# Eight PSUM banks of an attention stage dealt out anew: two for scores, three for maxima and transposed values

## The chip, the cores and the metric

The kernel runs on one core of one Trainium2 chip. The metric is the device time of the whole program in microseconds (us), the median of several runs.

## What is computed

One layer with two groups of heads over the same 2048 x 1024 input. Four heads are a gated DeltaNet (linear attention with a state that is carried from chunk to chunk); eight heads of 64 columns are forgetting attention. Both are gated, joined, projected out and normalised. The change concerns the attention alone:

```python
log_f = jax.nn.log_sigmoid(f_logit + f_bias)
cum = jnp.cumsum(jnp.moveaxis(log_f, 2, 1), axis=-1)
for i in range(s // Q_BLOCK):
    lo, hi = i * Q_BLOCK, (i + 1) * Q_BLOCK
    logits = (jnp.einsum('bhqd,bhkd->bhqk', q[:, :, lo:hi], k[:, :, :hi]) * scale
              + cum[:, :, lo:hi, None] - cum[:, :, None, :hi])
    logits = jnp.where(s_pos[None, :] <= t_pos[:, None], logits, -jnp.inf)
    p = jax.nn.softmax(logits, axis=-1)
    outs.append(jnp.einsum('bhqk,bhkd->bhqd', p, v[:, :, :hi]))
```

## The kernel before

Three stages follow one another: `project` (the input projection, convolutions, the inverses of the DeltaNet chunks), `mix` (the forgetting attention, with the DeltaNet chain woven in) and `project_out` (output projection and normalisation). Float32 products are made of three products of rounded parts, named hi and lo.

`mix` is written out slot by slot: every engine runs the same loop over slots `s` and does its share of slot `s` in an order fixed by hand. A slot is one of the 320 units (head, group of 512 queries, block of 128 keys). A *group* G is a head and 512 queries; there are 32. In slot `s` TensorE does, in this order:

- `scores(s)`: the transposed scores of unit s, 128 keys x 512 queries, into bank `st[s % ST]` by two matmuls (L1325, L1326), and a third (L1328) that masks a diagonal block;
- `values(s - 3)`: three matmuls (L1341, L1342, L1344) that add the unit of three slots ago (`LAG = 3`) to the output bank `pv`;
- the *aux items* of the slot: mostly one "max" item (L1294, with L1297 on a diagonal), a plain score tile whose row maxima are wanted for a later group; sometimes a "v" item (four transposes of the values, L1285) or a "row" item (L1300), which turns the maxima of a group, laid on a diagonal by GpSimd (`max_diag`, L1458), into a row;
- in eight slots of every nineteen one step of the DeltaNet chain (L1353 to L1394), in a bank of its own.

ScalarE reads the scores bank twice per slot (L1439 writes `p`, L1441 writes `p_hi`). GpSimd forms `p_lo` from the two (L1480), which the third matmul of `values` needs. VectorE reads the aux bank: a maximum over the columns (L1532) for a "max" item, two passes for a "v" item (L1519, L1521, then a semaphore increment at L1524), one for a "row" item (L1545, increment at L1547). It also does its part of the chain and, per group, the sums and rescaling, some of it behind DMAs (L1582 waits for the one that spreads the sums, L1588 for the one that brings the inverses back). SyncE issues all loads and stores of the stage in one queue.

Eight PSUM banks of 128 x 512 float32 are there: one for the chain, two for aux items, three for scores (`ST = 3`), two for output. Two waits guard them:

```python
done(pe, aux_used, m - 2)        # aux item m, L1278
done(pe, p_hi_ready, s - ST)     # scores of unit s, L1323
pe.wait_ge(p_hi_ready, s + 1)    # values of unit s, L1340
pe.wait_ge(p_lo_ready, s + 1)    # values of unit s, L1343
```

`done(eng, what, n)` waits until item n has been dealt with. So aux item m waits until VectorE has used item m - 2, and `scores(s)` until ScalarE has read unit s - 3, which `values(s - 3)` asks for right behind it.

Of the kernel before, what the change touches and what calls it, by code (L numbers as in the profile page):

```python
# [48 lines left out]
def flat(ap):  # L49
    return ap.rearrange("p a b -> p (a b)")  # L50
# [924 lines left out]
PER_HEAD = N_UNITS // FH  # L975
N_GROUPS = FH * NB
LAG = 3
ST, PH, PL = 3, 4, 3
LEAD = 20
SUM_AFTER, SCALE_AFTER = 2, 5  # L980
SPREAD, INVERT, GATHER, SPREAD_BACK, RESCALE = 1, 6, 7, 11, 16
# [68 lines left out]
def mix(nc, io, scr):  # L1050
    with ExitStack() as ctx:
# [3 lines left out]
        def bank(name):  # L1055
            return ctx.enter_context(nc.psum_tensor("m_" + name, [P, 512], F32))
# [46 lines left out]
        rb = bank("chain")  # L1103
        rb4 = rb[:].rearrange("p (h t) -> p h t", t=P)
        rb64 = rb[:, 0:GH * HALF].rearrange("p (h t) -> p h t", t=HALF)
        aux = [bank(f"aux{i}") for i in range(2)]
        st = [bank(f"st{i}") for i in range(ST)]
        pv = [bank(f"pv{i}") for i in range(2)]

# [29 lines left out]
        def done(eng, what, n):  # L1139

            if n >= 0:
                eng.wait_ge(what, n + 1)

        with nc.Block() as block:
# [123 lines left out]
            def _(pe):  # L1268
                def loaded(sems, i, n, each):

                    if n > 0:
                        pe.wait_ge(sems[i], each * n)

                def do_aux(item):
                    kind, *what = item
                    m = AUX_INDEX[item]
                    b = aux[m % 2]
                    done(pe, aux_used, m - 2)  # L1278
                    if kind == "v":
                        i, blk = what  # L1280
                        if blk == 0:
                            loaded([v_landed], 0, i, 16)
                        for j in range(4):
                            c = blk * 4 + j
                            mm = pe.transpose(b[:, j * P:(j + 1) * P], v_feat[:, c * P:(c + 1) * P], ident[:])  # L1285
                    elif kind == "max":
                        G, a, kb4 = what
                        h, g = divmod(G, NB)
                        if a == 0 and kb4 == 0:
                            loaded(QM_landed, G % 2, G // 2, 16)  # L1290
                            loaded(K2_landed, h % 2, (h + 1) // 2, 32)
                        diagonal = kb4 == g
                        n = max(a + 1, 2) * P if diagonal else 512
                        mm = pe.matmul(b[:, 0:n], QM[G % 2][:, a * P:(a + 1) * P],  # L1294
                                       K2[h % 2][:, kb4 * 512:kb4 * 512 + n], start=True, stop=not diagonal)
                        if diagonal:
                            mm = pe.matmul(b[:, a * P:n], ident_b[:], over_q[:, 0:n - a * P], start=False, stop=True)  # L1297
                    elif kind == "row":
                        pe.wait_ge(max_diag_ready, what[0] + 1)
                        mm = pe.matmul(b[0:1, :], ones_r[:], flat(max_diag[:]), start=True, stop=True)  # L1300
                    elif kind == "sum":
                        pe.wait_ge(den_ready, what[0] + 1)
                        for a in range(4):
                            mm = pe.matmul(b[:, a:a + 1], den[what[0] % 2][:, a * P:(a + 1) * P], ones[0:1, 0:1], start=True, stop=True)
                    else:
                        pe.wait_ge(rec_diag_ready, 1)
                        mm = pe.matmul(b[0:FD, :], ones[:], flat(rec_diag[:]), start=True, stop=True)
                    mm.then_inc(aux_ready, 1)
# [88 lines left out]
                for item in AUX_AT[-1]:  # L1397
                    if item[0] == "row":
                        pe.wait_ge(ones_set, 1)
                    do_aux(item)  # L1400
                for s in range(END_SLOT + 1):
                    if s < N_UNITS:
                        scores(s)
                    if 0 <= s - LAG < N_UNITS:
                        values(s - LAG)
                    for item in AUX_AT.get(s, ()):
                        do_aux(item)
                    if s in CHUNK_AT:
                        chain(*CHUNK_AT[s])
# [91 lines left out]
            def _(dve):  # L1501
                dve.wait_ge(ones_set, 1)

                def do_aux(item):
                    kind, *what = item
                    m = AUX_INDEX[item]
                    b = aux[m % 2]

                    def came():
                        dve.wait_ge(aux_ready, m + 1)  # L1510

                    if kind == "v":
                        i, blk = what
                        cut = slice(blk * 4, blk * 4 + 4)
                        src = b[:].rearrange("p (c h d) -> p c h d", c=4, h=2)
                        if blk == 0 and i >= 2:
                            dve.wait_ge(pv_done, 2 * PER_HEAD * (i - 1))
                        came()
                        dve.tensor_copy(v_hi[i % 2][:, cut, :, 0:FD], src).then_inc(v_hi_ready, 1)  # L1519
                        dve.wait_ge(v_hi_ready, 4 * i + blk + 1)  # L1520
                        dve.tensor_tensor(v_lo[i % 2][:, cut, :, :], src, v_hi[i % 2][:, cut, :, 0:FD].bitcast(F32), ALU.subtract)\  # L1521
                           .then_inc(v_ready, 1)
                        dve.wait_ge(v_ready, 4 * i + blk + 1)
                        dve.sem_inc(aux_used, 1)  # L1524
                    elif kind == "max":
                        G, a, kb4 = what
                        g = G % NB
                        n = max(a + 1, 2) * P if kb4 == g else 512
                        if a == 0 and kb4 == 0:
                            done(dve, mcol_ready, G - 1)  # L1530
                        came()
                        dve.reduce_max(maxima[:, a, kb4:kb4 + 1], b[:, 0:n], AX.X).then_inc(aux_used, 1)  # L1532
                        if a == 3 and kb4 == g:
                            dve.wait_ge(aux_used, m + 1)
                            done(dve, max_diag_ready, min(G - 1, ROWS_ON_PE - 1))
                            dve.reduce_max(mcol[:], maxima[:, :, 0:g + 1], AX.X).then_inc(mcol_ready, 1)
                            if G >= ROWS_ON_PE:
                                dve.wait_ge(mcol_ready, G + 1)
                                if G > ROWS_ON_PE:
                                    dve.wait_ge(max_row_stored, 16 * (G - ROWS_ON_PE))  # L1540
                                dve.tensor_scalar(neg_max[:], mcol[:].bitcast(F32), -1.0, None, ALU.mult).then_inc(neg_max_ready, 1)
                    elif kind == "row":
                        G = what[0]
                        came()
                        dve.tensor_scalar(Q2[G % 4][FD:FD + 1, :], b[0:1, :], -1.0, None, ALU.mult).then_inc(row_ready, 1)  # L1545
                        dve.wait_ge(row_ready, G + 1)
                        dve.sem_inc(aux_used, 1)  # L1547
                    elif kind == "sum":
                        G = what[0]
                        came()  # L1550
                        dve.reciprocal(rcol[:], b[:, 0:4]).then_inc(rcol_ready, 1)
                        dve.wait_ge(rcol_ready, 1)
                        dve.sem_inc(aux_used, 1)
                    else:
                        G = what[0]
                        if G >= 2:
                            dve.wait_ge(yb_stored[G % 2], 16 * (G // 2))
                        came()
                        dve.scalar_tensor_tensor(yb[G % 2][:], gated[G % 4][:], 0.5, b[0:FD, :], ALU.mult, ALU.mult)\
                           .then_inc(yb_ready, 1)  # L1560
                        dve.wait_ge(yb_ready, G + 1)
                        dve.sem_inc(aux_used, 1)
# [307 lines left out]
def build(nc, io, out):  # L1870
    def scratch(name, shape, dt=F32):
        return nc.dram_tensor("dram_" + name, shape, dt).ap()

    scr = {
        "feat": scratch("feat", (N_FEAT, P, SEQ)),
        "gates": scratch("gates", (GATES, SEQ)),
        "neg_cum": scratch("neg_cum", (FH, SEQ)),
        "mixT": scratch("mixT", (KT, P, SEQ)),
    }
    for n in ("q_hi", "q_lo", "k_hi", "k_lo"):  # L1880
        scr[n] = scratch(n, (4, P, SEQ))
    project(nc, io, scr)
    mix(nc, io, scr)
    project_out(nc, io, scr, out)
# [55 lines left out]
```

## Time and profile before

| | |
|---|---|
| median of 3 runs | 1650.15 us (1648.28 to 1652.33) |
| the profiled execution's own time | 1651.97 us |
| its span, first to last instruction | 1649.8 us |
| mean granted TensorE clock | 0.971 |
| `project` | until about 835 us |
| `mix` | about 835 to 1456 us |
| `project_out` | from about 1456 us |

The page of the profile gives the whole span, and the trace can be asked about any stretch: busy time by window, waits by what ended them, groups of instructions by line, and the instructions in order of time. PE is TensorE's matmuls, PEld its weight loads, DVE VectorE, ACT ScalarE, POOL GpSimd, SP SyncE's queue; a q behind an engine means its sequencer, as for the semaphore increments. The numbers in square brackets in a timeline are the idle time of the engine before the instruction and what ended it.

### The profile page before, as it was taken

Reading aid. Unit: us, or ns where it says so; the run is one execution under the profiler, and the core shown is the slowest. Engines: PE = TensorE matmul, PEld = TensorE weight load, DVE = VectorE, ACT = ScalarE, POOL = GpSimd, SP = SyncE. Lnnn points to the kernel's source line nnn. Section 1 sums busy time; section 2 is a strip of 40 time slices with the busy share of each in tenths; the row PEclk is TensorE's granted clock in tenths of the full one; section 3 lists DMA queues with packets and bytes.
Section 4 is the critical chain, followed back from the end, with each engine's and each line's share of the span. In section 5 each row is a group of like instructions: output and inputs, shape, how many; then the busy total and the mean of one; then the engine's idle time right before and its main releaser. Section 6 shows DMA issues by size and latency. Waiting matters only on the chain. (4 is left out here: it accounts for less than half of the span.)

```text
span 1649.8 us, 22201 instructions
## 1 busy us (share of the span) xinstructions
PE 1558.8 (94%) x7900; PEld 1230.7 (75%) x7900; DVE 924.2 (56%) x1436; ACT 691.6 (42%) x1307; POOL 625.5 (38%) x541
## 2 busy tenths in 40 slices
PE   6999999999979999999958999998999999979998
PEld 5888888888868888888836766766676677757886
DVE  7355555555348667301236676676577676544755
ACT  0346363645311111311115767765676777740100
POOL 2112121212201111111024877876786888911111
PEclk8999999999989999999968999999999999989999
DMA  6134334352683333226561646553545464233642
GB/s 247 45 112 132 105 118 126 96 141 83 149 101 128 116 127 124 74 78 135 152 173 35 170 118 164 154 145 91 147 123 144 130 164 156 62 115 101 193 140 89
DMA packets 190417, 206.35 MB, mean 125 GB/s; under 512 B 50764, under 2 KB 133964, under 8 KB 187276
## 3 DMA queue, kind: packets, MB, share of 16 engines
q1 hardware_dynamic: 189732, 203.11, 44.2%
q10 hardware_dynamic: 576, 1.84, 0.3%
q8 instruction: 63, 1.03, 0.3%
q14 instruction: 46, 0.38, 0.1%
HBM read 129.66 MB, written 75.17 MB: 124 GB/s over the span
## 5 line engine op out<-in xcount | busy, mean ns | idle before, releaser
L1480 POOL TENSOR_TENSOR m_p_lo<-m_p,m_p_hi 128x512 fp32r<-128x512 f32 (+1 forms) x320 | 373.9, 1191 | 81.7 <-ACT m_p_hi L1441 77.4
L537 PE MATMUL bank<-x_hi,w_hi 128*128 128x512 f32 x992 | 395.3, 398 | 8.5 <-DVEq L833 8.5
L537 PE MATMUL bank<-x_hi,w_lo 128*128 128x512 f32 x992 | 387.8, 391 | 0.0
L537 PE MATMUL bank<-x_lo,w_hi 128*128 128x512 f32 x992 | 386.9, 390 | 0.0
L562 POOL TENSOR_TENSOR w_lo<-w_raw,w_hi 128x512 fp32r<-128x512 f32 x66 | 98.9, 1519 | 506.8 <-ACT w_hi L618 506.8
L1439 ACT ACTIVATE m_p<-m_st,fcol 128x512 f32<-128x512 f32 (+1 forms) x320 | 204.1, 638 | 174.8 <-PE m_st L1326 93.1
L1532 DVE TENSOR_REDUCE m_maxima<-m_aux 128x1 f32<-128x512 f32 (+2 forms) x320 | 195.4, 619 | 137.3 <-PE m_aux L1294 87.6
L537 PEld LDWEIGHTS bank<-x_hi,w_hi 128*128 128x128 f32 x992 | 186.9, 188 | 44.9 <-issue 8.9
L537 PEld LDWEIGHTS bank<-x_hi,w_lo 128*128 128x128 f32 x992 | 186.6, 188 | 40.4
L537 PEld LDWEIGHTS bank<-x_lo,w_hi 128*128 128x128 f32 x992 | 187.2, 189 | 36.7
L1441 ACT ACTIVATE m_p_hi<-m_st,fcol 128x512 fp32r<-128x512 f32 (+1 forms) x320 | 202.5, 633 | 0.0
L860 DVE SCALAR_TENSOR_TENSOR bank<-arena,taps,bank 128x512 f32<-128x512 f32 x144 | 108.8, 756 | 75.9 <-ACT bank L661 72.5
L1341 PE MATMUL m_pv<-m_p_hi,m_v_hi 128*65 128x512 f32 (+1 forms) x320 | 124.4, 389 | 0.0
L1344 PE MATMUL m_pv<-m_p_lo,m_v_hi 128*65 128x512 f32 (+1 forms) x320 | 119.3, 373 | 4.4 <-POOL m_p_lo L1480 4.1
L830 DVE SCALAR_TENSOR_TENSOR ring<-ring,bank 128x512 f32<-128x512 f32 x32 | 21.9, 685 | 173.8 <-ACT ring L671 173.3
L1342 PE MATMUL m_pv<-m_p_hi,m_v_lo 128*64 128x512 f32 (+1 forms) x320 | 118.0, 369 | 0.0
L1325 PE MATMUL m_st<-m_Q,K 128*128 128x512 f32 x224 | 97.1, 434 | 0.0
L1294 PE MATMUL m_aux<-K,QM 66*128 66x512 f32 (+2 forms) x160 | 65.5, 422 | 29.7 <-DMA QM<-dram_q_hi 11.8
L1742 PE MATMUL o_bank<-o_w_hi,o_y_hi 128*128 128x512 f32 x256 | 81.3, 394 | 9.5 <-DVE o_y_lo L1796 9.5
L1734 POOL TENSOR_TENSOR o_rstd<-o_rstd,o_half 128x1 f32<-128x1 f32 x16 | 24.2, 1510 | 161.8 <-DVE o_rstd L1839 161.8
L674 ACT ACTIVATE ring<-bank 128x512 fp32r<-128x512 f32 x32 | 19.2, 598 | 152.3 <-PE bank L537 152.3
L1742 PE MATMUL o_bank<-o_w_lo,o_y_hi 128*128 128x512 f32 x256 | 80.9, 392 | 0.0
(204 smaller groups left out, 2550.6 us busy)
## 6 DMA issues: line engine op xcount, KB each, us to landing
w_raw<-in_w SPq DMA_DIRECT2D x31, 512.0 KB, 3.9
dram_feat<-ring SPq DMA_DIRECT2D x48, 256.0 KB, 3.6
arena<-dram_gates SPq DMA_DIRECT2D x32, 256.0 KB, 4.9
o_y<-dram_mixT SPq DMA_DIRECT2D x16, 512.0 KB, 6.0
o_x<-in_x SPq DMA_DIRECT2D x16, 512.0 KB, 4.0
out<-o_res SPq DMA_DIRECT2D x15, 512.0 KB, 4.9
arena<-in_xT SPq DMA_DIRECT2D x7, 1024.0 KB, 7.6
K<-dram_k_hi SPq DMA_DIRECT2D x12, 512.0 KB, 8.3
```

Source lines behind the costliest of these rows:

```text
L537: mm = pe.matmul(banks[bank_of(s)][:], w[:, i % 2, k * P:(k + 1) * P], x[:, k, b * BLOCK:(b + 1) * BLOCK], start=(k == 0 and n == 0), stop ...
L562: pool.tensor_tensor(w_lo[:, par, cut], w_raw[:, cut], w_hi[:, par, cut].bitcast(F32), ALU.subtract)\
L860: dve.scalar_tensor_tensor(own, src[:, 1 + i:1 + i + BLOCK], tap[:, i:i + 1], own, ALU.mult, ALU.add)\
L1325: pe.matmul(b[:, off:], K1[h % 2][:, keys], Q1[G % 4][:, off:], start=True, stop=False)
L1341: pe.matmul(b[0:FD + 1, off:], v_hi[i % 2][:, kb, j, :], p_hi[s % PH][:, off:], start=kb == 0, stop=False)
L1342: pe.matmul(b[0:FD, off:], v_lo[i % 2][:, kb, j, :], p_hi[s % PH][:, off:], start=False, stop=False)
L1344: pe.matmul(b[0:FD + 1, off:], v_hi[i % 2][:, kb, j, :], p_lo[s % PL][:, off:], start=False, stop=kb == 4 * g + 3).then_inc(pv_done, 1)
L1439: act.activation(p[s % PL][:, off:], st[s % ST][:, off:], ACT.Exp, bias=bias).then_inc(p_ready, 1)
L1441: act.activation(p_hi[s % PH][:, off:], st[s % ST][:, off:], ACT.Exp, bias=bias).then_inc(p_hi_ready, 1)
L1480: pool.tensor_tensor(p_lo[(s - 1) % PL][:, off:], p[(s - 1) % PL][:, off:], p_hi[(s - 1) % PH][:, off:].bitcast(F32), ALU.subtract).then_i ...
L1532: dve.reduce_max(maxima[:, a, kb4:kb4 + 1], b[:, 0:n], AX.X).then_inc(aux_used, 1)
L1742: mm = pe.matmul(banks[t % WIDE][:, cut], a[t % WIDE][:, k, :], b[:, k, cut], start=(k == 0 and n == 0), stop=(k == KT - 1 and n == 2))
```

## The change

One bank goes from the scores to the aux items. Aux item m takes bank `m % 3` and waits for item m - 3; `scores(s)` takes bank `s % 2` and waits until ScalarE has read unit s - 2. No instruction, transfer or order changes.

```diff
@@ -975,7 +975,8 @@
 LAG = 3
-ST, PH, PL = 3, 4, 3
+ST, PH, PL = 2, 4, 3
+AUX_BANKS = 3
 LEAD = 20
@@ -1103,7 +1104,7 @@
-        aux = [bank(f"aux{i}") for i in range(2)]
+        aux = [bank(f"aux{i}") for i in range(AUX_BANKS)]
         st = [bank(f"st{i}") for i in range(ST)]
         pv = [bank(f"pv{i}") for i in range(2)]
@@ -1274,8 +1275,8 @@
                 def do_aux(item):
                     kind, *what = item
                     m = AUX_INDEX[item]
-                    b = aux[m % 2]
-                    done(pe, aux_used, m - 2)
+                    b = aux[m % AUX_BANKS]
+                    done(pe, aux_used, m - AUX_BANKS)
@@ -1504,7 +1505,7 @@
                 def do_aux(item):
                     kind, *what = item
                     m = AUX_INDEX[item]
-                    b = aux[m % 2]
+                    b = aux[m % AUX_BANKS]
```

## Rows read from the trace of the kernel before

**Rows 1.** The page, part 1: busy time, share of the span, instructions.
```profile
PE 1558.8 (94%) x7900; PEld 1230.7 (75%) x7900; DVE 924.2 (56%) x1436; ACT 691.6 (42%) x1307; POOL 625.5 (38%) x541
```

**Rows 2.** Timeline near the start of the stage: start us, us, engine line op tiles.
```profile
868.06 1.19 PE L1294 MATMUL m_aux<-K,QM 66*128 66x512 f32 x2 [11.76 <-DMA QM<-dram_q_hi]
```

**Rows 3.** Busy time by window: PE, PEld, DVE, ACT, POOL, TensorE clock, DMA.
```profile
870.00:1449.00 579.00, 550.80 (x3177) 395.92 (x3175) 388.42 (x727) 398.80 (x744) 449.73 (x392) 0.98 0.47 128
1188.00:1192.00 4.00, 3.72 (x14) 2.81 (x15) 2.98 (x9) 0.84 (x2) 0.83 (x2) 0.57 0.43 124
1253.00:1257.00 4.00, 4.00 (x17) 3.31 (x16) 3.70 (x8) 1.63 (x3) 1.86 (x2) 0.57 1.00 281
1420.00:1449.00 29.00, 27.88 (x155) 19.51 (x153) 12.17 (x22) 24.02 (x46) 28.13 (x24) 1.00 0.19 51
```

**Rows 4.** Waits, 870 to 1449 us: total us, times, longest us.
```profile
POOL m_p_lo L1480 <- ACT m_p_hi L1441: 72.3, 56, 14.6
...
ACT m_p L1439 <- POOL m_p_lo L1480: 14.0, 16, 2.0
PEld m_aux L1294 <- DVE m_maxima L1532: 13.6, 23, 2.9
...
PEld m_aux L1294 <- DVEq L1524: 7.2, 6, 1.6
...
PE m_aux L1300 <- POOL m_max_diag L1458: 6.2, 10, 1.6
...
PE m_aux L1294 <- DVE m_maxima L1532: 5.5, 8, 2.4
...
PE m_aux L1294 <- DVEq L1524: 4.5, 6, 1.3
...
PE m_pv L1344 <- POOL m_p_lo L1480: 3.9, 6, 0.9
...
PE m_aux L1300 <- DVEq L1524: 1.0, 1, 1.0
PE m_aux L1294 <- DVEq L1547: 0.8, 2, 0.5
PE m_aux L1285 <- DVE m_maxima L1532: 0.7, 1, 0.7
```

**Rows 5.** Timeline behind a "v" item.
```profile
881.52 0.69 DVE L1521 TENSOR_TENSOR m_v_lo<-m_aux,m_v_hi 128x512 fp32r<-128x512 f32 x1
882.33 0.49 PE L1294 MATMUL m_aux<-K,QM 66*128 66x512 f32 x1 [1.33 <-DVEq L1524]
```

**Rows 6.** Timeline, 1181 to 1189 us: a short and a long aux wait.
```profile
1181.51 0.39 PE L1342 MATMUL m_pv<-m_p_hi,m_v_lo 128*64 128x512 f32 x1
...
1181.74 0.40 PE L1344 MATMUL m_pv<-m_p_lo,m_v_hi 128*65 128x512 f32 x1
...
1182.13 0.19 PEld L1294 LDWEIGHTS m_aux<-K,QM 66*128 66x128 f32 x1 [0.49 <-DVE m_maxima L1532]
1182.14 0.50 PE L1294 MATMUL m_aux<-K,QM 66*128 66x512 f32 x1
...
1187.47 0.19 DVE L1582 RECIPROCAL m_recs<-m_dens 64x8 f32<-64x8 f32 x1 [5.06 <-DMA m_dens<-m_den]
...
1188.28 0.61 PE L1294 MATMUL m_aux<-K,QM 66*128 66x512 f32 x1 [2.39 <-DVE m_maxima L1532]
```

**Rows 7.** Timeline: reads of units 94 and 95, loads for scores 96 and 97.
```profile
1037.06 0.68 ACT L1441 ACTIVATE m_p_hi<-m_st,fcol 128x512 fp32r<-128x512 f32 x1
...
1038.76 0.19 PEld L1325 LDWEIGHTS m_st<-m_Q,K 128*128 128x128 f32 x1
...
1039.18 0.68 ACT L1441 ACTIVATE m_p_hi<-m_st,fcol 128x512 fp32r<-128x512 f32 x1
...
1039.83 0.19 PEld L1325 LDWEIGHTS m_st<-m_Q,K 128*128 128x128 f32 x1
```

**Rows 8.** Groups by shape, 870 to 1449 us: busy us, mean ns.
```profile
L1480 POOL TENSOR_TENSOR m_p_lo<-m_p,m_p_hi 128x512 fp32r<-128x512 f32 x223 | 290.7, 1325 | 60.5 <-ACT m_p_hi L1441 59.1 <-PE m_pv L1344 1.0
```

## The prediction

> **What bounds the kernel.** I read the page's busy shares first: TensorE is busy for 94% of the span, no other engine for more than 56% [rows 1]. Only `mix` holds the banks in question, so I then asked for busy time by window there. Its first 35 us end in a wait of 11.76 us for a load of queries [rows 2], which SyncE issues behind the chunk loads; what is saved before 868 us runs into that wait, and I count nothing there. That leaves 870 to 1449 us, 579 us for nearly all of the 320 slots. Matmuls are in flight for 550.8 of them, GpSimd works for 449.7, ScalarE 398.8, VectorE 388.4 [rows 3]. So TensorE's order is the clock of the stage, GpSimd is a second one close behind, and in the last 29 us, where no aux items are left, GpSimd is full (28.1 of 29) [rows 3].
>
> The view of waits says what TensorE loses. Of the waits on `aux` banks, those ended by VectorE, L1532, or by its increments at L1524 and L1547, are waits for a bank; those ended by GpSimd's `max_diag` are for data, as are those for `p_lo` [rows 4]. The waits for a bank are 5.5 + 4.5 + 1.0 + 0.8 + 0.7 = 12.5 us in 18 places. The timeline shows their two kinds. A "v" item holds its bank for two passes and the second ends 0.1 us before TensorE goes on [rows 5]. Or VectorE, which works in order, is itself held: for 5.06 us by the DMA that spreads the sums, and TensorE then stands for 2.39 us because two maxima are unread [rows 6].
>
> **What the third aux bank gives.** A stall costs more than its row says. Back-to-back matmuls of 512 columns start 0.23 us apart but are recorded with 0.39 to 0.40 us [rows 6], so the first 0.17 us of each stall are hidden under the matmul before: at 1182.14 us the matmul has no idle time of its own, though its weight load waited 0.49 us for the bank and it starts 0.40 us behind the one before it, in place of 0.23. With 0.17 us for each of 18 stalls I get 12.5 + 3.1 = 15.6 us. The weight loads' waits of the same kind are, for the max items alone, 13.6 + 7.2 = 20.8 us in 29 places [rows 4]; with the row items there are about a dozen places more than in the matmul rows, which give at most 0.17 us each, about 2 us in all. I take 17.5 us as what TensorE loses for want of a bank; the bounds are 12.5 us (the matmul rows) and 20.8 us (the load rows).
>
> Is one bank more enough? I went through the places in the timeline. In each, item m - 3 had been used at least 0.8 us before item m - 2, and where the gap was longer than that, before TensorE stood still at all; so the wait itself goes in every place. Part of it comes back one or two items later, which in their turn wait for item m - 2. That happens where the next item follows closely or the gap is long: about 0.5 us of the 2.39 us at 1188 us, 0.7 us of the 1.33 us at 882 us, some 0.2 us in all elsewhere. Take off 1.5 us.
>
> **What other waits take back.** The "row" items wait for `max_diag`, 6.2 us in 10 places [rows 4]. That comes from VectorE's last maximum of the group through GpSimd, so TensorE, once it comes earlier, waits longer there. Five of the saved stalls sit right ahead of a row item that is already waiting or nearly so, with some 2.5 us between them. Take off 2.5 us. `values` waits for `p_lo`: 3.9 us of matmul rows in 6 places [rows 4]. For each saved stall I looked for the next slot in which `p_lo` came last and asked whether GpSimd had stood idle for ScalarE in between by as much as was saved; then GpSimd moves up too and the gain is kept. It had in nearly all: such idle time is 72.3 us in 56 places [rows 4], and a full `p_lo` takes 1.3 us [rows 8] of a mean slot of 1.9 us (607 us over 320). About 1.5 us fall between saved stall and a full GpSimd. Since several waits act together, I take 3 us for it. Bounds: nothing, and all of the gain.
>
> **What the lost scores bank costs.** `scores(s)` used to ask for unit s - 3, which `values(s - 3)` asked for anyway, so that wait never bound. Now it asks for unit s - 2, one slot fresher, and at the head of the slot: behind it in TensorE's queue stand the three matmuls of `values(s - 3)`, the aux items and the chain step, and so VectorE's maxima too. Its price can be read without running it: the end of ScalarE's second read of unit s - 2 against the start of the weight load of `scores(s)`. The read of unit 94 ended at 1037.74 us and scores 96 began at 1038.76, a slack of 1.0 us; that of unit 95 ended at 1039.86 and scores 97 had begun at 1039.83, the tightest of all [rows 7]. Over the 318 pairs the median slack is 1.55 us; 3 are under 0.06 us, 10 under 0.31, 25 under 0.56, 66 under 1.06. As the trace stands, the new wait costs 0.2 us in all. The saved stalls do not pull it tight: in the slots right behind them, where TensorE will now come earlier by the stall, the slack less the stall is at least 0.68 us. But TensorE as a whole runs a little nearer to ScalarE, whose own wait for `p_lo` is 14.0 us in 16 places [rows 4]. If every slack shrinks by 0.25 us the wait costs 1.9 us; by 0.5 us, 6.3; by 0.75 us, 14.1. I take 1.5 us; bounds 0.2 and 14.
>
> **The clock.** The granted clock is 0.57 in the 4 us at 1188 us, that is the lower level of 1.2 GHz for most of them, right behind the 2.39 us stall, and 0.57 again in the 4 us at 1253 us, behind two shorter ones [rows 3, 6]. 0.57 over 4 us is 3.4 us at half speed, which costs up to 1.7 us each time. I count 1.5 us for both together, bounds 0 and 3.4. The Trainium skill, "TensorE: Matmul & The Clock Gate", section "HAM oscillation — how this bites in real kernels", prices throttled time at its half as well, and reports of another kernel that double-buffering PSUM gave no further gain once its waits for DMA were dealt with. By that sentence the sum would be zero; that is the second rival below. The trace speaks for a gain here, since TensorE waits for VectorE at these banks and not for a load.
>
> **The sum.** 17.5 - 1.5 - 2.5 - 3 - 1.5 + 1.5 = 10.5 us less. The profiled execution took 1651.97 us, so 1641.5 us; the median of the runs is 1.8 us below that execution, so 1639.7 us. Everything outside of `mix` is untouched: `project_out` starts earlier by the same amount. That part is gained in full, as its first transfers (weights, first values) are issued from slots of `mix` that move up too.
>
> **The rivals.**
>
> *GpSimd or the "row" items take it back.* The stage is nearly balanced: GpSimd's busy time and its waits for VectorE leave it perhaps a tenth of the stage. If that slack is in the wrong places, TensorE meets `p_lo` and `max_diag` instead of the bank. For it: the last 29 us, and the 10 row waits. Against it: the 72.3 us in which GpSimd waits for ScalarE. Then `p_lo` waits grow by what bank waits lose, and the gain is 2 to 4 us: about 1647 us.
>
> *A third bank only moves the wait.* If VectorE's lateness is what counts, TensorE gets one item ahead and then stands at the next. For it: the 5.06 us in which VectorE waits for a DMA. Against it: of 18 stalls only one is longer than a whole slot of 1.9 us. It gives no more than the matmul rows less half, some 3 us: 1647 us as well.
>
> *Scores become the wait: slower.* ScalarE is held in some slots by a chain step or by `p_lo`, and TensorE now stands at the head of the slot, with the aux matmuls behind it; VectorE gets its maxima later and the row items follow. It decides once the mean slack falls by about 0.75 us: 14 us lost against the 12 gained, and a little more for lower clocks behind new stalls. For it: 25 slots under 0.56 us, many of them in the last 29 us. Against it: the median of 1.55 us, and at least 0.68 us behind each saved stall. Price at a shrinkage of 0.9 us: some 20 us lost, 1657 us.
>
> That the change does nothing is not a case: both sides of the aux ring and of the scores ring turn with the new numbers.
>
> **How the numbers follow.** The forecast has 0.62, with its own range 1634 to 1645 us. The first rival (GpSimd and the rows) has 0.12, the second (the wait moves on) 0.10, the slower one 0.12, and 0.04 are left for a larger gain. 0.3% is 5 us, about what a measurement of this kernel can tell from no change. Some of the forecast's own low end (a gain under 5 us) goes to "same": faster 0.64, same 0.23, slower 0.13. The range takes in the forecast's own and the rivals without gain and leaves out most of the slower one: 1632 to 1653 us.
>
> **What the profile after will show.** Right: waits of TensorE on `aux` ended by L1532, L1524 and L1547 fall from 12.5 us (18 places) to 3 us or less; the row waits grow from 6.2 to some 8 us, the `p_lo` waits from 3.9 to some 6 us; a new wait of L1325 for ScalarE's L1441 of 1 to 2 us in matmul rows; TensorE's busy time nearly as before, `mix` 10 to 12 us shorter, and no low clock at 1188 us. Wrong: L1325 waits of 5 us or more, many in slots with a chain step; or `p_lo` waits up by 8 us; or VectorE's waits for its two DMAs grown, since SyncE's single queue issues them no sooner.

## The result, and the profile after

The changed kernel took 1631.72 us in the median of 4 runs (1624.73 to 1636.19), the kernel before 1650.33 us (4 runs): a ratio of 0.988, 95% interval [0.985, 0.992], or 18.6 us less by the medians. That is the way the forecast pointed, but 1.8 times its 10.5 us, and 0.3 us below its range. Two further comparisons, made on other occasions with the experiments below, gave 0.9925 [0.9895, 0.9955] and 0.9933 [0.9902, 0.9964], medians of 1635.02 and 1632.97 us, both inside the range. Weighted by their intervals the three ratios give 0.9917, some 13.6 us. So the change is worth 11 to 19 us, and the first comparison is the largest of three. Over all runs of the two kernels (58 in four comparisons and 18 in three) the medians are 1647.98 and 1633.73 us, 14.3 us apart.

In the lines of the changed kernel everything behind L978 is one number higher: L1295 is the max item's matmul, L1301 the row item's, L1326 the first of the scores, L1345 the one that needs `p_lo`. Its profiled execution took 1624.73 us, the fastest of its four. Busy time by window in it, the 4 us at the two places where the clock was low before, then the stretch that answers to 870 to 1449 us, as in [rows 3]:

```profile
1164.00:1168.00 4.00, 2.79 (x16) 1.81 (x15) 2.35 (x8) 1.56 (x4) 3.44 (x4) 1.00 0.76 200
1228.00:1232.00 4.00, 4.00 (x26) 2.97 (x25) 3.66 (x8) 2.88 (x5) 3.15 (x4) 1.00 0.97 222
860.00:1421.00 561.00, 540.52 (x3171) 392.48 (x3171) 386.86 (x725) 397.59 (x742) 449.75 (x393) 0.99 0.48 132
```

Both places have the full clock in this execution.
GpSimd, ScalarE and VectorE work as long as before, in a stretch that is 18 us shorter. The waits of TensorE in that stretch, to be held against [rows 4]:

```profile
PE m_aux L1301 <- POOL m_max_diag L1459: 7.6, 11, 1.7
PE m_pv L1345 <- POOL m_p_lo L1481: 5.5, 8, 1.3
PE m_aux L1295 <- issue: 3.5, 1, 3.5
PE m_aux L1295 <- DVE m_maxima L1533: 1.7, 5, 0.6
...
PE m_aux L1301 <- DVE m_maxima L1533: 0.5, 1, 0.5
PE m_aux L1295 <- DVEq L1525: 0.4, 1, 0.4
```

The waits for a bank are 1.7 + 0.5 + 0.4 = 2.6 us in 7 places, before 12.5 us in 18. No wait of L1326 for ScalarE is listed. The view of that line shows one stop alone in front of the scores in 320 slots, 0.3 us, for a row of maxima:

```profile
its engine sat idle before it (us, times) until:
  DVE Q L1546: 0.3, 1
```

The views list no idle time under 0.15 us. Instruction by instruction, three scores items (slots 95, 203 and 317) begin their weight load 0.05 us behind ScalarE's read of the unit two slots earlier, where they had begun 0.04 us ahead of its end, 0.01 us and 0.00 us behind it: this is also the median distance in the one-bank kernel further on, where the items do wait. So these three wait for the bank, for 0.2 us in all.

The place of the 2.39 us stall [rows 6] looks like this after:

```profile
1165.42 0.40 PE L1345 MATMUL m_pv<-m_p_lo,m_v_hi 128*65 128x512 f32 x1
1165.65 0.20 DVE L1583 RECIPROCAL m_recs<-m_dens 64x8 f32<-64x8 f32 x1 [4.34 <-DMA m_dens<-m_den]
...
1166.45 0.38 PE L1295 MATMUL m_aux<-K,QM 66*128 66x256 f32 x1 [0.63 <-DVE m_maxima L1533]
...
1167.49 1.16 PE L1372 MATMUL m_chain<-m_R,m_XT 128*128 128x128 f32 x8 [0.58 <-DVE m_R L1600]
```

VectorE is held by the same DMA, for 4.34 us. TensorE gets one item further, then meets the bank for 0.63 us at the next one, where I had put about 0.5 us, and VectorE again at a chain step for 0.58 us, which I had not.

**Where the time went.** From the starts of the same instructions in the two traces I took five marks: the first max item, the first matmul of scores 4, 15 and 319, and the first matmul of the output projection. Times are us from the first max item; "first max" is from the start of the span. The rows below "changed" are other executions of the same kernel and the experiments, told further on.

| kernel | first max | scores 4 | scores 15 | scores 319 | 15 to 319 | output |
|---|---|---|---|---|---|---|
| before | 835.0 | 34.1 | 58.6 | 612.5 | 553.9 | 629.2 |
| changed | 825.0 | 32.1 | 52.8 | 594.2 | 541.4 | 611.8 |
| changed, 2nd | 831.0 | 32.4 | 53.6 | 597.7 | 544.1 | 614.7 |
| changed, 3rd | 834.6 | 33.8 | 56.7 | 601.2 | 544.6 | 618.2 |
| two and two | 836.0 | 33.6 | 58.4 | 612.9 | 554.5 | 629.8 |
| third only early | 834.5 | 33.4 | 58.1 | 611.5 | 553.4 | 628.9 |
| third only late | 828.8 | 33.3 | 56.1 | 602.6 | 546.5 | 619.5 |
| rows later | 833.3 | 32.7 | 53.7 | 600.5 | 546.8 | 617.5 |
| before, queries first | 829.5 | 22.7 | 47.6 | 602.6 | 555.0 | 618.8 |
| changed, queries first | 835.9 | 19.4 | 42.8 | 588.1 | 545.3 | 605.5 |
| the same, 2nd | 830.6 | 19.4 | 42.7 | 584.9 | 542.2 | 601.2 |

The two profiled executions of the result differ by 27 us (1651.97 and 1624.73 us). Ten of them lie ahead of the first max item, in `project`, whose code is the same in all: the first max item behind it starts anywhere from 825 to 836 us, for kernels with two aux banks and with three alike. `mix` itself is 17.4 us shorter to the first matmul of the output projection.

### The profile page after: what moved, and what is told of

Read it like the earlier page. It is cut to its first block and busy times, and to the rows that moved or that the text cites. A ratio compares the mean times of both kernels' runs of the same rounds, so it can differ in the third digit from the quotient of the medians.

```text
span 1622.5 us, 22201 instructions
## 1 busy us (share of the span) xinstructions
PE 1547.4 (95%) x7900; PEld 1226.9 (76%) x7900; DVE 923.2 (57%) x1436; ACT 691.5 (43%) x1307; POOL 624.3 (38%) x541
## 5 line engine op out<-in xcount | busy, mean ns | idle before, releaser
L537 PE MATMUL bank<-x_hi,w_hi 128*128 128x512 f32 x992 | 395.1, 398 | 3.3 <-DVEq L833 3.3
L537 PE MATMUL bank<-x_hi,w_lo 128*128 128x512 f32 x992 | 387.6, 391 | 0.0
L537 PE MATMUL bank<-x_lo,w_hi 128*128 128x512 f32 x992 | 386.7, 390 | 0.0
L1533 DVE TENSOR_REDUCE m_maxima<-m_aux 128x1 f32<-128x512 f32 (+2 forms) x320 | 194.4, 618 | 122.1 <-PE m_aux L1295 77.1
L537 PEld LDWEIGHTS bank<-x_hi,w_lo 128*128 128x128 f32 x992 | 186.5, 188 | 40.5
L537 PEld LDWEIGHTS bank<-x_hi,w_hi 128*128 128x128 f32 x992 | 186.8, 188 | 39.7 <-issue 3.7
L537 PEld LDWEIGHTS bank<-x_lo,w_hi 128*128 128x128 f32 x992 | 187.0, 189 | 36.3
L1345 PE MATMUL m_pv<-m_p_lo,m_v_hi 128*65 128x512 f32 (+1 forms) x320 | 119.1, 372 | 5.8 <-POOL m_p_lo L1481 5.5
L1326 PE MATMUL m_st<-m_Q,K 128*128 128x512 f32 x224 | 97.3, 434 | 0.0
L1295 PE MATMUL m_aux<-K,QM 66*128 66x512 f32 (+2 forms) x160 | 61.3, 400 | 22.5 <-DMA QM<-dram_q_hi 12.9
```

What stands on the lines that cost most here:

```text
L537: mm = pe.matmul(banks[bank_of(s)][:], w[:, i % 2, k * P:(k + 1) * P], x[:, k, b * BLOCK:(b + 1) * BLOCK], start=(k == 0 and n == 0), stop ...
L1326: pe.matmul(b[:, off:], K1[h % 2][:, keys], Q1[G % 4][:, off:], start=True, stop=False)
L1345: pe.matmul(b[0:FD + 1, off:], v_hi[i % 2][:, kb, j, :], p_lo[s % PL][:, off:], start=False, stop=kb == 4 * g + 3).then_inc(pv_done, 1)
```

## Experiments

**Which part of the change, and which part of the stage.** Four kernels on one chip, with 23 runs of the kernel before. First the changed kernel again.

> The changed kernel once more, on one chip with the three below. Theory A (the stage itself is shorter by what the waits for a bank took, and project differs between executions by chance): 17 to 18 us faster than before, the interval a few us wide; the stage from its first maximum to slot 319 takes 594 us, before 612. Rival (part of the 18.6 us is chance in project): 10 to 14 us faster.

1635.02 us in the median of 6 runs against 1648.13 us, ratio 0.9925 [0.9895, 0.9955], some 12 us. The stage took 597.7 us to scores 319. The rival is nearer: part of the 18.6 us had been chance.

Then the loss of the scores bank alone.

```diff
-AUX_BANKS = 3
+AUX_BANKS = 2
```

> Two banks for scores, two for aux items, one bank left idle: the loss of the scores bank alone. Theory A (two banks for scores cost nothing, the reads of unit s - 2 are done in time): within 1 us of before, 18 us slower than the changed kernel. Rival (the loss costs some 5 us and the third aux bank gives 23): 5 us slower than before, with waits of scores for ScalarE in the trace.

1649.01 us (12 runs), ratio 1.000 [0.998, 1.002]: within 4 us of before, and 14 us above the changed kernel. The stage took 612.9 us to scores 319, before 612.5, and its waits of TensorE between 871 and 1450 us are nearly those of before, with none for ScalarE in front of the scores. The first five lines:

```profile
PE m_aux L1295 <- DVE m_maxima L1533: 5.4, 6, 2.9
PE m_aux L1301 <- POOL m_max_diag L1459: 5.0, 9, 1.6
PE m_aux L1295 <- issue: 4.6, 1, 4.6
PE m_aux L1295 <- DVEq L1525: 4.4, 6, 1.3
PE m_pv L1345 <- POOL m_p_lo L1481: 3.9, 6, 0.9
```

So nothing that these runs can tell is paid for the bank taken away, and the gain is that of the bank given.

Third and fourth, the depth of the wait was parted from the number of banks: three banks throughout, but in one part of the stage an item still waits for m - 2.

```diff
-                    done(pe, aux_used, m - AUX_BANKS)
+                    done(pe, aux_used, m - (AUX_BANKS if m < AUX_INDEX["max", 2, 0, 0] else AUX_BANKS - 1))
```

> Banks as in the changed kernel, but from the first maximum of group 2 on an aux item waits for item m - 2 again; the third bank is used only in the first four slots. My prediction's step (what is saved before the load of group 2's queries runs into that wait): 0 us against before. Theory A (the slots behind it profit too, since the clock rises sooner and SyncE issues sooner): 2 to 3 us faster than before.

1646.26 us (12 runs), ratio 0.9986 [0.9965, 1.0007]. By the medians it is 1.9 us faster than before, and the interval runs from 5.8 us faster to 1.2 us slower: my prediction's 0 us and the 2 to 3 us of theory A both lie in it, and the run doesn't decide between them. In the trace most of the early saving is lost. Slot 3 begins 4.3 us earlier than before, and slot 4 only 0.6 us earlier, because in between stands the wait for the load of queries, before 11.76 us [rows 2], here

```profile
PE m_aux L1295 <- DMA QM<-dram_q_hi: 14.5, 1, 14.5
```

The fourth is the reverse:

```diff
-                    done(pe, aux_used, m - AUX_BANKS)
+                    done(pe, aux_used, m - (AUX_BANKS - 1 if m < AUX_INDEX["max", 2, 0, 0] else AUX_BANKS))
```

> The reverse: in the first four slots item m waits for m - 2, from the first maximum of group 2 on for m - 3. My prediction's step: as fast as the changed kernel. Theory A: 15 us faster than before, 2 to 3 us slower than the changed kernel. Rival (what one part gives is lost in the other, so the two do not add up): less than 12 us faster.

1635.9 us (6 runs), ratio 0.9921 [0.9893, 0.9950], against 1635.02 us and 0.9925 of the changed kernel on the same chip. The measurable gain is that of the third bank from the first max item of group 2 on, as the prediction has it. Whether the early part adds nothing or the 2 to 3 us of theory A is again less than the intervals can tell (0.9 us between the two medians).

**Where the price of a scores bank begins, and whether a fourth aux bank is worth something.** Scores in one bank, once with three aux banks (one left idle) and once with four.

```diff
-ST, PH, PL = 2, 4, 3
+ST, PH, PL = 1, 4, 3
```

> Scores in one bank, aux items in three, one bank idle: scores of unit s wait until ScalarE has read unit s - 1. It shows where the price of a scores bank begins. Theory A (two banks are free because ScalarE's reads end 1.5 us before they are asked for, in the median, and a slot lasts 1.9 us): with one bank that margin is gone in nearly every slot, some 0.5 to 1 us a slot, so 150 to 350 us slower than the changed kernel. Rival (TensorE has so much other work per slot that ScalarE stays hidden): less than 30 us slower.

1740.37 us (3 runs), ratio 1.057 [1.053, 1.061]: 105 us slower than the changed kernel, under my 150 to 350 us and far over the rival's 30. Half of the slots pay, and they pay in the new place:

```profile
PE m_st L1326 <- ACT m_p_hi L1442: 78.6, 154, 1.2
PE m_aux L1295 <- DMA QM<-dram_q_hi: 13.8, 1, 13.8
PE m_aux L1301 <- POOL m_max_diag L1459: 4.0, 3, 2.2
...
PE m_pv L1345 <- POOL m_p_lo L1481: 0.6, 1, 0.6
```

78.6 us in 154 slots are 0.51 us each by the matmul rows. The other 26 us would be 0.17 us more for each of them, what the prediction takes as the part of a stall that such a row doesn't show; no run tests this by itself, and the waits that went away leave room for more. Behind the stop for the load, the other waits have nearly gone, `p_lo` among them: a TensorE that is held at the scores no longer meets GpSimd. The second differs in one line more, `AUX_BANKS = 4`:

> Scores in one bank, aux items in four. Only the difference to the kernel with one and three tells something, the worth of a fourth aux bank. Theory A (VectorE's lateness is covered by three): within 3 us of it. Rival (depth of the aux ring still counts): 5 to 10 us faster than it.

1743.11 us (3 runs), ratio 1.058 [1.054, 1.062], 2.7 us above the kernel with one and three. A fourth aux bank gives nothing beside one scores bank. Since that bound hides most of the aux waits in both, this doesn't show what a fourth would give beside two.

**The waits that are left.** The row items wait for GpSimd's diagonal; two slots later they should find it ready.

```diff
-            put(min(slot_of(n - 1) + 2, first_unit(G) - 1) if G else -1, ("row", G))
+            put(min(slot_of(n - 1) + 4, first_unit(G) - 1) if G else -1, ("row", G))
```

> The changed kernel with each row item two slots later, where the next group leaves room. Theory A (the saved bank waits went on in part as waits of the row items for GpSimd's diagonal of maxima, 11.1 us in 13 places after the change): these fall to 2 us or less and the kernel is 6 to 9 us faster than the changed one. Rival (TensorE meets p_lo next, GpSimd being nearly full): p_lo waits grow by as much and the time stays within 2 us.

1635.88 us (11 runs), ratio 0.9934 [0.9912, 0.9955]; the changed kernel had 0.9925 and 0.9933. No gain. The edit does what it says and the time turns up elsewhere, between 866 and 1437 us:

```profile
PE m_pv L1345 <- POOL m_p_lo L1481: 9.0, 17, 1.4
PE m_st L1326 <- DVE m_Q L1546: 4.6, 5, 1.1
...
PE m_aux L1295 <- DVE m_maxima L1533: 3.8, 5, 2.2
```

The row waits fall to none in this stretch, from 7.6 us. But `p_lo` is waited for 9.0 us in 17 places, before the edit 5.5 in 8; in five groups the row is now late for its scores, 4.6 us; and the waits for a bank ended by L1533 are 3.8 us, before the edit 1.7. The rival has the time right. Of its mechanism, that `p_lo` takes it all, the trace shows less than half: 3.5 us of some 10.

**The stop in the first slots.** SyncE issues the load of group 2's queries behind 9 loads for each of two chunks and the keys of head 1. Here it stands ahead of them; the loads are the same.

```diff
+                sp.wait_ge(mcol_ready, 1)
+                load_max_queries(2)
                 sp.wait_ge(XT_zeroed, 1)
                 for n in range(2):
...
-                        if G + 2 < N_GROUPS and s == MAX_SLOT[G] + 2:
+                        if 0 < G and G + 2 < N_GROUPS and s == MAX_SLOT[G] + 2:
```

> The changed kernel with the load of group 2's queries for the maxima issued by SyncE before the chunk loads instead of behind them. Theory A (the stop of 12.9 us in the first slots is the place of this load in SyncE's queue, and swallows what the third bank saves there): the stop falls to 1 to 3 us and the kernel is 8 to 11 us faster than the changed one. Rival (behind it the next load of that queue, queries for the scores or group 3's, is as late): 0 to 3 us faster.

1620.27 us (5 runs), ratio 0.9856 [0.9820, 0.9891], some 24 us less than before and, by the ratios, some 11 us less than the changed kernel: theory A at its upper end. The stop is gone from the list altogether; in `mix` what leads it now is

```profile
PE m_aux L1303 <- POOL m_max_diag L1461: 11.4, 14, 2.2
...
PE m_pv L1347 <- POOL m_p_lo L1483: 5.5, 8, 1.3
PE m_aux L1297 <- issue: 4.7, 1, 4.7
```

and scores 4 starts 19.4 us behind the first max item, where it was 32 to 34 us.

The third line is worth a look, for it stands in the lists of all kernels, as one stop of 3.5 to 4.8 us, and none of these edits touches it. It comes at slot 144, the first max item of group 17. The profile names nothing for it, but in the kernel before SyncE issues that group's queries behind nine chunk loads (1127.88 to 1132.68 us), and they land 5.1 us after their issue, as TensorE goes on:

```profile
1133.69 0.59 SPq L1158 DMA_DIRECT2D QM<-dram_q_hi  x1
...
1138.87 0.77 PE L1294 MATMUL m_aux<-K,QM 66*128 66x512 f32 x1 [4.66 <-issue]
```

So it is the same kind of stop. It is the longest one left in the stage, and in all thirteen traces 6.8 us at the lower clock level begin in it. No run moved this load.

To see whether the two edits add up, the load was moved in the kernel before as well, and both were run on one chip with the changed kernel and 16 runs of before.

> The kernel before (two aux banks, three for scores) with the load of group 2's queries issued before the chunk loads. Theory A (the bank change and the place of the load are two separate things, and only the first four slots are hidden under the stop for that load): 9 to 11 us faster than before, and the changed kernel with the same edit another 15 to 18 us faster than this one, 3 us more than the two differ without the edit, since the early saving now counts. Rival (the early saving counts already): the two differ by as much as without the edit.

1635.01 us (9 runs), ratio 0.9932 [0.9908, 0.9957]. The early saving is seen in the marks: scores 4 at 22.7 us with two aux banks and at 19.4 us with three, 3.3 us between them; with the stop in place the two had differed by 0.3 to 2.0 us. In the whole time it doesn't stand out: theory A had the changed kernel with the same edit 15 to 18 us below this one, and it is 10.6 us below (the next two).

> The changed kernel a third time, to stand on one chip beside the two with the load moved. The stage from first maximum to slot 319 took 594.2 and 597.7 us in two executions, 612.5 before. Theory A: 594 to 598 us again and 13 to 16 us faster than before. If the first result was chance in the other stages: 10 us or less.

1632.97 us (8 runs), ratio 0.9933 [0.9902, 0.9964], some 11 us, under theory A's 13 to 16. By the marks it is the slowest of the three executions, 601.2 us to scores 319, outside of the 594 to 598 that I expected.

> The changed kernel with the load moved, again. Theory A: 23 to 27 us faster than before, 9 to 11 us faster than the changed kernel. Rival (the first result, 1.4% against before and 0.9% against the changed kernel's own re-run, was flattered by fast executions): 18 us or less.

1624.43 us (6 runs), ratio 0.9860 [0.9827, 0.9894], some 23 us; 8.5 us below the changed kernel's median (12 us by the ratios) and 10.6 us below that of the kernel before with the load moved. This is the fastest kernel of the study, ahead of both, in two comparisons. The bank change is worth about 11 us with the load moved and 11 to 19 without: each edit brings its own part. The extra 3 us that theory A expected of the two together don't show; they lie within what these runs can tell.

## Where the prediction was right, and which step failed

**What bounds the stage; the gain lies in the bank waits behind 868 us.** Right, and shown within what the runs can tell: with the third bank used only there, the kernel is as fast as the changed one (1635.9 and 1635.02 us); used only before, it is not measurably faster than before (ratio 0.9986 [0.9965, 1.0007]), and the stop for the load grows from 11.76 to 14.5 us.

**17.5 us lost for want of a bank, 1.5 of them come back.** The waits for a bank are 2.6 us after (1.7 and 3.3 us in the other two executions), where at most 3 us were forecast. The start of each scores item in the two traces shows the stalls go one by one: 1.4 us at slot 136, 2.7 us at 171, 1.4 us at 216. The matmul rows before showed 1.14, 2.39 and 1.14 us; that a row hides some 0.2 us of a stall is borne out by these three, by 0.26 to 0.33 us.

**Row items, 2.5 us back.** Their waits grew from 6.2 to 7.6 us, in the other executions to 8.1 and 7.9, about the 8 us forecast: 1.4 to 1.9 us, where I took off 2.5.

**GpSimd, 3 us back.** The `p_lo` waits grew from 3.9 to 5.5 us, and one of them costs twice. At slot 49 TensorE came earlier by three saved stalls, met `p_lo`, and its clock fell behind the wait (0.57 in 942 to 946 us, the lower level for most of it; 1.00 there before):

```profile
941.03 0.45 PE L1345 MATMUL m_pv<-m_p_lo,m_v_hi 128*65 128x512 f32 x1 [1.26 <-POOL m_p_lo L1481]
```

```profile
942.00:946.00 4.00, 4.00 (x21) 2.89 (x18) 0.99 (x2) 1.76 (x4) 4.00 (x4) 0.57 0.80 237
```

Slots 49 and 50 gave back 2.0 to 2.5 us in all three executions of the changed kernel, the largest return of all. So 3 us was about the size, by a smaller wait and a clock that I had not counted.

**Scores, 1.5 us.** Wrong in size: 0.2 us. Two and two took as long as before, and in the changed kernel three scores items waited for ScalarE, for 0.2 us together. The slack that I read ahead, 0.2 us short in all with every read in its old place, was the better estimate than the 1.5 us that I put in its place: the median slack after is 1.51 us, before 1.55, so it hardly shrank.

**The clock, 1.5 us gained.** Not shown to be the change's. The low clock at 1253 us is gone in all three executions (1.6 us at slots 207 and 208), but it is gone in two and two and in third only early as well, where items there wait for m - 2 and the stalls ahead of it stay. That at 1188 us is gone in the first, while the other two have a low stretch of 3.4 us near it. With the new one at slot 50, TensorE is at the lower level between slots 15 and 319 for 10.2, 17.1 and 13.7 us in the three, before for 13.7: on the whole nothing. The Trainium skill ("TensorE: Matmul & The Clock Gate", section "HAM oscillation — how this bites in real kernels") prices such time at half of it; the 1.6 us for 3.4 us at half speed agree.

**The rivals.** That a third bank only moves the wait is refuted by the 12.5 us that became 2.6. That GpSimd and the rows take it back holds for 3 to 4 us, by their waits and the clock at slot 50. That scores become the wait is refuted for two banks and true for one, where the price is 105 us: the edge lies between, with 1.5 us of median slack at two and a slot of 1.9 us between one and two.

**Why 18.6 us and not 10.5.** From slot 15 on the terms give 8.9 us, as 1.6 of the 10.5 lie in slots 4 to 14; measured were 9.3, 9.8 and 12.5 us (third, second and first execution). The 1.5 us for scores belong there. So do some 1.2 us of the 12.5: the stop at slot 144 lasted 3.45 us in the first execution and 4.66 us before, for a load and not for a bank. The third execution has them too (3.54 us), and gives 2.2 us back at slots 172 and 173, around its low clock. Ahead of slot 15 I had 1.6 us and the three executions have 5.8, 5.0 and 1.9, first to third. Of the excess of the first two over the third, 1.4 to 1.7 us are there at scores 4 already, since the load of queries lands sooner: the stop ends 31.1, 31.4 and 32.8 us behind the first max item, before 33.1. The other 1.6 to 2.2 us come with a clock that rises sooner behind the stop. In the 10 us from scores 4 on, for before, the changed kernel, its second and its third execution:

```profile
869.00:879.00 10.00, 10.00 (x33) 7.20 (x32) 6.20 (x11) 5.07 (x8) 3.86 (x4) 0.55 0.03 7
```

```profile
857.00:867.00 10.00, 9.72 (x44) 6.71 (x42) 7.24 (x13) 6.33 (x10) 5.14 (x4) 0.83 0.05 15
```

```profile
863.00:873.00 10.00, 9.73 (x40) 6.86 (x39) 7.05 (x12) 5.66 (x10) 5.14 (x4) 0.76 0.05 15
```

```profile
868.00:878.00 10.00, 10.00 (x31) 7.13 (x29) 5.99 (x10) 4.88 (x8) 3.82 (x3) 0.52 0.01 1
```

The third is the same kernel as the two ahead of it, with the clock of before: so the change alone does not bring it. Together the marks to scores 319 give 11.3, 14.8 and 18.3 us. On top of that comes `project`, whose end moves by up to 11 us between executions.

The step that failed is therefore the range, and in the sum the part ahead of 868 us. The range, "The forecast has 0.62, with its own range 1634 to 1645 us" and 1632 us at the low end of the whole, was made of the bounds of my terms alone. The same text says that 0.3%, 5 us, is about what a measurement can tell, and no term carries it: the 4 runs before had a median 2.4 us above that of all 58, the 4 runs after one 2.0 us below that of all 18, so by this measure 4.3 us of the 18.6 are chance. The sum put what is saved ahead of the stop at nothing ("what is saved before 868 us runs into that wait, and I count nothing there") and had no term for the clock behind it; up to slot 15 the runs showed 1.9 to 5.8 us in place of its 1.6. The third term mis-sized is that of the scores wait, 1.5 us for 0.2. What moved 0.3 us past the range cannot be told apart among them. Whether the sooner clock is likelier with the third bank is open: with the stop in place, the clock rose 3.4 to 4.5 us behind the start of scores 4 in five of six profiled executions that wait for m - 3 or m - 4 throughout, and 8.8 to 9.5 us behind it in the sixth and in all four that wait for m - 2 somewhere. One against five is too few to call it chance or cause.

## What to carry to other kernels

A bank is worth what TensorE waits for it at one reader, and costs what the other reader's slack falls short: both can be read from one trace, instruction by instruction, before anything is built. Here the slack, measured in every slot, told the price of the lost bank (0.2 us), and what I added to it out of caution was wrong. And before a range is given, look at how much the untouched stages move between executions; here that was more than the terms in dispute.

## What the hardware showed that I had not expected

The first stage, whose code never changed, ended its last matmul anywhere from 821.5 to 832.5 us after the start of the span in thirteen profiled executions. In the pair of the result, 8 of the 10 us lie in waits of TensorE there: 8.5 us at one place (L537 for VectorE's increment at L833) became 3.3, and 3.6 us at L524 for GpSimd's weights became 0.3. And a wait of 1.26 us at slot 48 was followed, 1.4 to 2.0 us later, by 3.4 us at TensorE's lower clock level in all three executions of the changed kernel, while no such stretch followed the waits of 1.33 and 1.14 us (slots 8, 135 and 215) in the kernel before. The length of the wait alone doesn't decide: one of 1.65 us at slot 165 is in all three executions, and right behind it the clock fell in the second only.
